# Moving weight differences and row weighting of the routing stretch to GpSimd, and roundings on ScalarE ahead

## The reference, cut to what matters

```python
x = x + merged @ w_out
h = rms_norm(x, g_ffn)
g_prob = softmax(h @ w_group + b_group)          # 4 groups
g_idx = argmax(g_prob)
e_prob = softmax((h @ w_expert)[g_idx] + b_expert)   # 8 experts of that group
top_p, top_i = top_k(e_prob, 2)
top_w = g_gate * top_p / sum(top_p)
for e in range(32):
    hid = silu(h @ w_gate[e]) * (h @ w_up[e])
    out += combine[:, e] * (hid @ w_down[e])
x = x + out
```

## Time and profile before

| what | value |
|---|---|
| median of 3 runs | 2525.36 us (2524.77 to 2529.39) |
| the profiled execution's own time | 2529.46 us |
| its span | 2527.5 us |
| TensorE busy | 2315.9 us, 92% |
| VectorE busy | 1484.9 us, 59% |
| ScalarE busy | 1155.2 us, 46% |
| GpSimd busy | 424.7 us, 17% |

### The profile page before, as it was taken

One profiled execution on the slowest core, in us unless ns is written; L12 is line 12 of the kernel. 1 busy time (PEld: TensorE's weight loads), 2 busy tenths in 40 slices (PEclk: granted clock), 3 DMA queues, 4 the chain that ended last, 5 costly groups with the idle time before them and its releaser, 6 DMA issues.

```text
span 2527.5 us, 29085 instructions
## 1 busy us (share of the span) xinstructions
PE 2315.9 (92%) x9901; PEld 1652.8 (65%) x9901; DVE 1484.9 (59%) x1501; ACT 1155.2 (46%) x1173; POOL 424.7 (17%) x151
## 2 busy tenths in 40 slices
PE   6899895999999999989988889999899988889997
PEld 4344544665665665658877766788688776667886
DVE  6948337888888888855545434455455464424554
ACT  4112414667667667643324546433343244464432
POOL 2640000000000000010005455400100053555000
PEclk8899997999999999999989899999999998999999
DMA  5233242899999999945543233555355332434652
GB/s 211 67 117 127 73 168 110 333 364 367 364 362 366 363 362 367 374 167 191 179 146 102 84 127 130 174 184 185 118 184 196 128 128 82 133 117 138 201 184 93
DMA packets 166450, 496.80 MB, mean 197 GB/s; under 512 B 10272, under 2 KB 21792, under 8 KB 136400
## 3 DMA queue, kind: packets, MB, share of 16 engines
q1 hardware_dynamic: 164528, 491.70, 54.9%
q10 hardware_dynamic: 1616, 3.24, 0.4%
q0 software_dynamic: 208, 0.59, 0.1%
HBM read 494.45 MB, written 1.05 MB: 196 GB/s over the span
## 4 chain that ended last, share of the span: by engine, by line
PE 63%; issue 14%; DVE 12%; POOL 6%; ACT 3%; DVEq 0%; DMA 0%; ACTq 0%; POOLq 0%
PE ps L967 11%; PE ps L968 11%; PE ps L969 11%; PE ps L1347 9%; POOL w_lo L3041 6%; PE ps L1328 5%; PE ps L1332 5%; PE ps L1018 4%; PE ps L1038 1%; PE ps L1316 1%; PE ps L1109 1%; PE ps L1385 1%; DVE W_r L2704 1%; ACT w_hi L1790 1%; PE ps L1364 1%
## 5 line engine op out<-in xcount | busy, mean ns | idle before, releaser
L3041 POOL TENSOR_TENSOR w_lo<-raw,w_hi 128x2048 fp32r<-128x2048 f32 x72 | 334.9, 4669 | 1599.7 <-ACT w_hi L1592 1404.5
L1592 ACT ACTIVATE w_hi<-raw 128x2048 fp32r<-128x2048 f32 (+1 forms) x204 | 379.0, 1866 | 459.2 <-PE ps L969 417.9
L967 PE MATMUL ps<-w_hi,a_hi 128*128 128x512 f32 (+1 forms) x1216 | 476.6, 392 | 54.6 <-POOL w_lo L3041 29.8
L968 PE MATMUL ps<-w_lo,a_hi 128*128 128x512 f32 (+1 forms) x1216 | 467.1, 384 | 0.0
L969 PE MATMUL ps<-w_hi,a_lo 128*128 128x512 f32 (+1 forms) x1216 | 465.1, 383 | 0.0
L2065 DVE TENSOR_TENSOR w_lo<-raw,w_hi 128x2048 fp32r<-128x2048 f32 (+1 forms) x132 | 293.1, 2227 | 264.8 <-ACT w_hi L1592 257.5
L967 PEld LDWEIGHTS ps<-w_hi,a_hi 128*128 128x128 f32 x1216 | 235.8, 194 | 105.7 <-POOL w_lo L3041 32.5
L969 PEld LDWEIGHTS ps<-w_hi,a_lo 128*128 128x128 f32 x1216 | 235.4, 194 | 44.5
L968 PEld LDWEIGHTS ps<-w_lo,a_hi 128*128 128x128 f32 x1216 | 236.3, 194 | 40.9
L1328 PE MATMUL ps<-w_hi,W_r 128*128 128x512 f32 x468 | 190.8, 408 | 5.4 <-DVE w_lo L2704 4.7
L967 PE MATMUL ps<-w_hi,y_hi 128*128 128x512 f32 x384 | 156.6, 408 | 18.4 <-DVEq L2530 18.4
(11 more groups left out here) (403 smaller groups left out, 3692.4 us busy)
## 6 DMA issues: line engine op xcount, KB each, us to landing
raw<-in_w_in SPq DMA_DIRECT2D x56, 1024.0 KB, 5.1
raw<-in_ffn_w_gate SPq DMA_DIRECT2D x44, 1024.0 KB, 5.1
raw<-in_ffn_w_up SPq DMA_DIRECT2D x44, 1024.0 KB, 5.1
raw<-in_ffn_w_down SPq DMA_DIRECT2D x40, 1024.0 KB, 5.0
raw<-in_w_up SPq DMA_DIRECT2D x30, 1024.0 KB, 7.9
raw<-in_w_gate SPq DMA_DIRECT2D x30, 1024.0 KB, 7.0
lo_f<-in_w_up SPq DMA_DIRECT2D x30, 1024.0 KB, 8.1
lo_f<-in_w_down SPq DMA_DIRECT2D x29, 1024.0 KB, 7.6
```

The source lines that it names most:

```text
L967: pe.matmul(dst, a_h, b_h, start=first, stop=False, **kw)
L968: pe.matmul(dst, a_h, b_l, start=False, stop=False, **kw)
L1592: act.activation(E.view(w_hi, name), E.view(raw, name), ACT.Copy).then_inc(hi_split, 1)
L3041: pool.tensor_tensor(E.view(w_lo, name), E.view(raw, name), E.view(w_hi, name).bitcast(F32), ALU.subtract)\
```

## The change

- TensorE's broadcast of the gain into rows moves from behind `turn_residual("f", ...)` to behind memory attention, and VectorE's two copies of it to behind its memory attention, ahead of the gates. They use two of the small banks there, not banks 4 and 5.
- The four instructions L2503 go. In their place ScalarE scales x by `rstd` into `xn`, two instructions of 128 x 1024, with the columns put in order (signal `scaled`), and GpSimd multiplies `xn` with `gain_row` in place, two of 128 x 1024 (signal `normed`).
- ScalarE's roundings of the rows move into `route`, one ahead of each exponential.
- The lower part of the rows goes from VectorE to GpSimd, two of 128 x 1024.
- ScalarE rounds both halves of g first and half 0 of u first ahead of the statistics of x.
- GpSimd makes the lower halves of g first (ahead of the rows), u first and g second (behind them), six of 128 x 2048. VectorE keeps those of the loop, and waits ahead of them until the six are counted.
- GpSimd no longer waits for the residual; its four loads come behind its new work.
- VectorE's memset of `hid_e` moves behind `spots`.

```diff
@@ tensor
+            for h in range(2):
+                dst = bank(("gain_row", h))
+                for k in range(4):
+                    m = pe.matmul(dst[:, k * P:k * P + P], gain["f"]..., ident, start=True, stop=True)
+                fill(m, ("gain_row", h))
             for i, br in ((1, "dsa"), (2, "mem")):
...
             turn_residual("f", "wo")
-            for h in range(2):
-                dst = bank(("gain_row", h))
...
@@ scalar
+            for name, half in ((("g", "first"), 0), (("g", "first"), 1), (("u", "first"), 0)):
+                expert_rounded(name, half)
             act.wait_ge(done["residual"], nth("residual", ("wo", 1, 1)))
             stats("f", x_sb, junk_f)
             for t in range(2):
+                act.activation(xn[:, t].rearrange("p (h k s) -> p h k s", h=2, k=4),
+                               x_sb[:, t].rearrange("p (h s k) -> p h k s", h=2, k=4), ACT.Copy,
+                               scale=r_of["f"][:, t:t + 1]).then_inc(done["scaled"], 1)
+                act.wait_ge(done["scaled"], nth("scaled", t))
+
+            def row_rounded(t):
                 act.wait_ge(done["normed"], nth("normed", t))
                 act.activation(h_rows[0][:, t], xn[:, t], ACT.Copy).then_inc(done["row_hi"], 1)
...
             def route():
+                row_rounded(0)
                 act.wait_ge(done["route_in"], nth("route_in", 0))
                 act.activation(rts(0, 4), rts(0, 4), ACT.Exp).then_inc(done["route"], 1)
                 act.wait_ge(done["route"], nth("route", "exp"))
+                row_rounded(1)
                 act.wait_ge(done["route_in"], nth("route_in", 1))
...
                 route()
-                expert_rounded(("g", "first"), 0)
-                expert_rounded(("g", "first"), 1)
+                expert_rounded(("u", "first"), 1)
                 for kb in range(1, KB, 2):
                     gathered_copy(("G", "first", 0, kb), kb, 0)
-                expert_rounded(("u", "first"), 0)
-                expert_rounded(("u", "first"), 1)
@@ vector
             attention("mem", 2, float(P) ** -0.5, None, probs, 2)
+            for h in range(2):
+                name = ("gain_row", h)
+                dve.wait_ge(bank_filled[bank_of[name]], fills(name))
+                dve.tensor_copy(gain_row[:, 512 * h:512 * h + 512]..., psum(name)...)
...
-            dve.wait_ge(done["rstd"], nth("rstd", "f"))
-            for t in range(2):
-                for h in range(2):
-                    ins = stt(out=xn..., in0=by_part(x_sb...), scalar=r_of["f"][:, t:t + 1], in1=gain_row...,
...
             def route():
+                dve.wait_ge(done["rstd"], nth("rstd", "f"))
...
-                for t in range(2):
-                    dve.wait_ge(done["row_hi"], nth("row_hi", t))
-                    tt(h_rows[1][:, t], xn[:, t], h_rows[0][:, t].bitcast(F32), ALU.subtract)...
-                dve.memset(hid_e[SLOTS:P], 0.0).then_inc(vector_step, 1)
...
-                expert_lower(("g", "first"), 0)
-                expert_lower(("g", "first"), 1)
                 spots()
-                expert_lower(("u", "first"), 0)
-                expert_lower(("u", "first"), 1)
+                dve.wait_ge(done["row_lo"], nth("row_lo", 1))
+                dve.memset(hid_e[SLOTS:P], 0.0).then_inc(vector_step, 1)
...
-                expert_lower(("g", "second"), 0)
                 halves_added(("first", "u"), bank_of[("u", "first")], fills(("u", "first")), low_u)
                 hidden_rows("first", slice(0, 1))
-                expert_lower(("g", "second"), 1)
+                dve.wait_ge(expert_lo, 2 * len(FIRST_TILES))
@@ gpsimd
-            pool.wait_ge(done["residual"], nth("residual", ("wo", 1, 1)))
+            def expert_lower(name, half):
+                u = (name, half)
+                pool.wait_ge(expert_hi, E.split_number(u) + 1)
+                pool.tensor_tensor(E.expert_raw(u)[1], E.expert_raw(u)[0], E.expert_hi(u).bitcast(F32), ALU.subtract)\
+                    .then_inc(expert_lo, 1)
+
+            expert_lower(("g", "first"), 0)
+            expert_lower(("g", "first"), 1)
+            for t in range(2):
+                pool.wait_ge(done["scaled"], nth("scaled", t))
+                pool.tensor_tensor(xn[:, t], xn[:, t], gain_row, ALU.mult).then_inc(done["normed"], 1)
+                pool.wait_ge(done["normed"], nth("normed", t))
+            for t in range(2):
+                pool.wait_ge(done["row_hi"], nth("row_hi", t))
+                pool.tensor_tensor(h_rows[1][:, t], xn[:, t], h_rows[0][:, t].bitcast(F32), ALU.subtract)\
+                    .then_inc(done["row_lo"], 1)
+                pool.wait_ge(done["row_lo"], nth("row_lo", t))
+            for name in (("u", "first"), ("g", "second")):
+                for half in range(2):
+                    expert_lower(name, half)
```

More of the change, by code:

```diff
@@ L62 @@
            "relued maxed exped probs probs_turned branch gates residual route_in route silu hidden "
-           "hidden_turned masks places spots tables normed row_hi row_lo picked gathered gathered_act lower summed gated "
+           "hidden_turned masks places spots tables scaled normed row_hi row_lo picked gathered gathered_act lower summed gated "
            "expert_hidden expert_turned spread out_hi out_split scattered gate_ln decay decay_exp decayed gk_turned masked state columns").split()
@@ L240, in plan @@
     attention("mem", 2)
+    for h in range(2):
+        small(("gain_row", h))
+    mark("scaled", 0, 1)
     mark("gates", "ssm", "dsa", "mem")
@@ L256, in plan @@
         fill(("fT", hh, t), b)
-    for h in range(2):
-        fill(("gain_row", h), 4 + h)
     mark("route_in", 0, 1); mark("route", "exp", "expert")
@@ L1245, in _ @@
                       lambda h, s_: vm_sb[:, s_, h * P:h * P + P], probsT, probs, up_ssm)
+            for h in range(2):
+                dst = bank(("gain_row", h))
+                for k in range(4):
+                    m = pe.matmul(dst[:, k * P:k * P + P], gain["f"][:, 4 * h + k:4 * h + k + 1].broadcast_to([P, P]), ident,
+                                  start=True, stop=True)
+                fill(m, ("gain_row", h))
             for i, br in ((1, "dsa"), (2, "mem")):
@@ L2426, in _ @@
             attention("mem", 2, float(P) ** -0.5, None, probs, 2)
+            for h in range(2):
+                name = ("gain_row", h)
+                dve.wait_ge(bank_filled[bank_of[name]], fills(name))
+                dve.tensor_copy(gain_row[:, 512 * h:512 * h + 512].rearrange("p (k s) -> p k s", k=4),
+                                psum(name).rearrange("p (s k) -> p k s", k=4)).then_inc(bank_freed[bank_of[name]], 1)
+                dve.wait_ge(bank_freed[bank_of[name]], fills(name))
             for i, br in enumerate(("ssm", "dsa", "mem")):
@@ L2590, in route @@
                 tt(rts(7, 1), rts(6, 1), rts(5, 1), ALU.mult).then_inc(vector_step, 1)
-                dve.wait_ge(vector_step, step.next())
-                for t in range(2):
-                    dve.wait_ge(done["row_hi"], nth("row_hi", t))
-                    tt(h_rows[1][:, t], xn[:, t], h_rows[0][:, t].bitcast(F32), ALU.subtract).then_inc(done["row_lo"], 1)
-                    dve.wait_ge(done["row_lo"], nth("row_lo", t))
-                dve.memset(hid_e[SLOTS:P], 0.0).then_inc(vector_step, 1)
                 dve.wait_ge(vector_step, step.next())
@@ L2777, in experts @@
                     gathered(("G", "first", 0, kb), ("first", 0, kb), kb, 0)
-                expert_lower(("g", "first"), 0)
-                expert_lower(("g", "first"), 1)
                 spots()
-                expert_lower(("u", "first"), 0)
-                expert_lower(("u", "first"), 1)
+                dve.wait_ge(done["row_lo"], nth("row_lo", 1))
+                dve.memset(hid_e[SLOTS:P], 0.0).then_inc(vector_step, 1)
+                dve.wait_ge(vector_step, step.next())
                 evacuate("token_rows", place_rows.rearrange("p j s -> p (j s)"), psum("token_rows"))
```

## The result

The changed kernel takes **2538.11 us** (median of 6 runs, 2536.7 to 2539.99) against 2525.51 us of the kernel before (6 runs, 2521.66 to 2529.39): 1.0047 times as long, 95% interval 1.0037 to 1.0058. It is slower, by some 12 us, where 10.5 were forecast; the two ranges of single launches don't meet. The profiled executions differ by 10.6 us (spans 2538.1 and 2527.5), and nearly all of that is there when the loop over the tiles begins.

A forecast was written before the change was run, and what follows sets the result against it. Ahead of the loop, VectorE's chain of tiny instructions was taken to set the time almost alone. Terms 0.9 + 7.3 + 2.3 = +10.5 us on the 2525.36 us median gave 2535.9 us, range 2525 to 2540.

The forecast's parts named there:

- exclusion with turns: In routing, two-input SBUF instructions of VectorE and GpSimd exclude each other whole and alternate: +10.5 us, chance 0.80.
- Rival A: No exclusion in the routing, so VectorE simply loses the work taken off it: -6.7 us, 2518.7 us, chance 0.11.
- rival B: In routing VectorE wins each time it asks and GpSimd falls behind: -6 to +2, 2522 us taken, chance 0.09.
- The broadcast: Behind memory attention, the moved broadcast delays TensorE, no longer hidden: +0.9 us, bounds 0 and 2.1.
- The logits, "-3.4": At the start of `route`, the first reduction comes with the logits at 389.4 instead of 392.77: -3.4 us.
- ScalarE's scaling: Ahead of GpSimd's products, ScalarE's 128x1024 scaling into `xn` takes 1.6 us, at most 2.32; first half done at 389.0.
- rival C: A deeper loss: scaling at 2.32 us starts everything 0.7 later, slow clock phases add 1.7: 2538 us; no separate chance.
- The fifth GpSimd instruction's release of VectorE: In `route`, five GpSimd instructions in a row end at 404.0, with VectorE then at L2555: +9.8 us.
- The instruction held behind it: Behind the ranks' copy, GpSimd's u first half 1 holds VectorE at L2608 or L2611 until 414.3: +11.7 us.
- `spots`: Behind the gather, with two lower halves gone (4.4 us), `spots` and TensorE's L1420 come +7.3 us.
- g first and g second: Ahead of the loop, TensorE waits for g second's lower half, 4.59 us instead of 4.50 / 2: +2.3 us.
- the soft place: At g first, after 3.8 us rest, TensorE's clock falls (+10.5, chance 0.47) or stays up (+8.2, 2533.6 us, 0.33).

The follow-up runs named there:

- experiment 2: Changed kernel, but ScalarE rounds and GpSimd lowers both halves of u first ahead of the statistics, right behind g first: 2530.55 us, ratio 1.001.
- 3 to 5: Kernel before, with GpSimd busy on a spare 128x512 area from the statistics on: 10 subtractions 2534.5 us, 20 copies 2530.18 us, 30 zeroings 2527.84 us.
- Experiment 6: Kernel before with only the gain's broadcast and its two copies moved behind memory attention: 2528.13 us, ratio 1.0001.
- experiment 7: Changed kernel with the gain's broadcast and its two copies back at their old place: 2540.27 us, ratio 1.0043.

## Why the prediction held, and where it was off

**The mechanism** was right: exclusion with turns, five GpSimd instructions in a row that let VectorE go at 404.0, an instruction held by each of the last four (the first came before VectorE had its logits), one more held at L2594. Experiments 2 and 3 to 5 show it apart from the rest of the change. Rival A (no exclusion) is refuted by the 1.86 to 4.40 us of the held instructions, rival B (VectorE wins) too: GpSimd's products took 2.4 us each throughout.

**Step by step**, in the traces. After's statistics begin 0.1 us later than before's, which is taken off here.

1. The broadcast: +0.9 forecast. From the start of memory attention's last product to the next up projection 3.65 us (318.89 to 322.54) against 3.08 (319.29 to 322.37): +0.57. Experiment 6 can't tell its total from that of before. What I had missed is that it was a cover for TensorE's clock at its old place.
2. The logits, "-3.4": **this step failed.** The first reduction came at 392.48, 0.4 earlier than before instead of 3.4, since TensorE's clock fell and the logits took 6.29 us. By experiment 7 that cost 0.5 us, not 3: VectorE would only have waited for GpSimd instead. The sum didn't need the step; I had booked no gain from it, but I took it as the time from which VectorE fills GpSimd's gaps.
3. ScalarE's scaling: 1.6 us forecast, 4.28 / 2 = 2.14 measured, close to the bound of 2.32 and twice the contiguous 1.06. GpSimd began at 389.7 for 389.1. The rule of the Trainium skill that the prediction set beside rival C (page "Advanced Engine Details and Errata", section "SBUF Cachelines") agrees with the 2.14.
4. The fifth GpSimd instruction's release of VectorE: 404.0 forecast, 403.9 measured. GpSimd's 2.4 us for 128x1024 was right; its 4.50 for 128x2048 is 0.1 below what I took, and the turns cost nothing visible on its side. That VectorE stood at the instruction I had named (L2555 of before, L2547 now) is luck: it lost one turn to the late logits, and L2537 slipped through without one. In experiment 7, without the late logits, it was one held instruction further.
5. The ranks' copy: 409.7 forecast, 409.5 measured.
6. The instruction held behind it: ends at 414.3 forecast, 414.1 measured. I had named L2608 or L2611 of before; it is the first, a TENSOR_SCALAR with one input, and the rule that I wrote down (two operands) would not have named it.
7. `spots`: +7.3 forecast, +8.3 measured (429.57 - 0.1 - 421.20). The missing 1.0 is in the gather: its products start 0.43 us apart for 4.4 us (419.75 to 424.15) in the changed kernel, for 1.8 (408.13 to 409.96) in the one before, and 0.24 apart behind that. The clock rose later, and VectorE's first instruction behind the gather came 8.5 us after L1409 instead of 7.35. That is rival C's slow clock, 1.0 of its 1.7 us.
8. g first and g second: +2.3 forecast, +1.9 measured (460.42 - 450.18 = 10.2 at L1347, less 8.4 at L1420). It is made of three: from L1420 to the end of u first TensorE gained 1.0 us (the end is 7.3 later, the start 8.4), the two waits for g second's lower halves are 2.2 us longer in all (2.7 + 4.9 for 0.7 + 4.7), and 0.7 went to a slower clock behind them.

**TensorE's clock**, the soft place: g first now begins at full clock, after 3.8 us of rest, and the clock falls soon after (0.90, then 0.76 in the windows shown, against 0.50 in the earlier trace rows). It is neither of my two cases, but one between them: 1.0 us of the 2.3 that I had set on it.

The sum in the trace is 0.1 at the statistics (the 0.57 of the broadcast, against 0.40 by which memory attention's last product already began earlier, and 0.07 on the way), 8.3 and 1.9: 10.2 us at the loop, 10.6 at the end, 10.5 forecast. That this fits to 0.3 us is partly luck: the broadcast came 0.3 under its term, `spots` 1.0 over and g second 0.4 under. The ratio makes it 11.9, and the rest of 1.3 is inside its interval (9.3 to 14.6 us).

## What to carry to other kernels

Before you hand GpSimd a long instruction to relieve VectorE, look at what VectorE does at the same time: a chain of tiny instructions with two SBUF inputs advances by about one for each GpSimd instruction that reads SBUF, so each can cost the whole of that one; the stretch in which VectorE read PSUM and one SBUF operand was free, and there the same move gave 3.8 us. Work that seems out of place on an engine may be what keeps its clock up, so ask what rests when it is gone. And look beyond the stretch: nearly all of a gain of 9 us was lost again at two places, 1,300 and 2,000 us later, where a wait grew by 0.36 us and TensorE's clock was lower behind it.

## What the runs showed of the hardware

- The exclusion lasts for the rest of GpSimd's instruction, however small VectorE's is: 128x8 elements took 1.86 to 2.21 us beside GpSimd's of 2.35, and a CAST of 128x8 to integers took 4.56 us beside one of 4.54 in the changed kernel (0.17 where it began first, in experiment 2).
- GpSimd's zeroing leaves two-input instructions alone (0.17 to 0.23 us) but holds a TENSOR_SCALAR of 8 or 32 elements (0.42 and 0.52 us instead of 0.17 and 0.18); one of 2 elements was not held (0.17).
- ScalarE reads 1024 elements at a step of 16 bytes in 2.14 us, side by side in 1.06.
- TensorE's clock after a rest: 32 small products took 3.76 us behind 0.5 us of rest and 6.3 to 7.0 behind 2.6 us; in block three the clock stayed full behind 2.85 us and had a mean of 0.86 behind 3.21.
